# Modulation units two at a time between the mixer's projections, in a fused two-model forward pass

## The reference

```python
mod = jax.nn.silu(c) @ w_ada[l] + b_ada[l]
sh1, sc1, g1, sh2, sc2, g2 = jnp.split(mod, 6, axis=-1)
h = modulate(x, norm1_g[l], sh1, sc1)       # rms_norm * (1+sc) + sh
q_a, k_a, v_a, qk_m, v_m, o_m, gates = jnp.split(h @ w_in[l], offs, axis=-1)
attn = head_rms_norm(moba_attention(rope(q_a), rope(k_a), v_a), attn_out_g[l], 8)
q_m, k_m = jnp.split(silu(causal_conv(qk_m, conv_w[l], conv_b[l])), 2, axis=-1)
hm = mlstm_chunkwise(q_m, k_m * dh ** -0.5, v_m, i_pre, f_pre)  # num / max(|den|, exp(-m))
hm = head_rms_norm(hm, mlstm_out_g[l], 4) * sigmoid(o_m)
x = x + g1 * (concatenate([attn, hm]) @ w_out[l])
h2 = modulate(x, norm2_g[l], sh2, sc2)
x = rms_norm(x + g2 * hier_moe(h2, ...), norm_f_g)   # top group of 4, top 2 of its 8 experts
for i in range(2):                                   # the second model's layers
    x = x + gate1 * (diff_attention(h) if i == 0 else axial_gqa(h))
    x = x + gate2 * ((silu(h @ w_gate) * (h @ w_up)) @ w_down)
return rmsnorm(x, final_g)
```

## Time and profile before

| what | value |
|---|---|
| median of 3 runs | 1418.47 us |
| the profiled execution | 1423.29 us, of which the span of its instructions is 1421.5 us |
| PE busy | 1170.6 us (82% of the span), 9691 instructions |
| PEld busy | 931.3 us (66%) |
| DVE, ACT busy | 617.6 us (43%), 527.2 us (37%) |
| chain that ended last | PE 56%, DMA 22%, DVE 13%, ACT 8%, issue 2% |
| read from memory | 394.97 MB, 279 GB/s over the span |

### The profile page before, as it was taken

How to read it: one execution, slowest core, us unless ns; L and a number is a source line. 1 busy time by engine, 2 the same in 40 slices (tenths; PEclk the granted TensorE clock), 3 DMA queues, 4 the chain that set the end, 5 groups by cost and what they waited for, 6 DMA issues and landing times.

```text
span 1421.5 us, 22433 instructions
## 1 busy us (share of the span) xinstructions
PE 1170.6 (82%) x9691; PEld 931.3 (66%) x9691; DVE 617.6 (43%) x1358; ACT 527.2 (37%) x1154; POOL 0.2 (0%) x4
## 2 busy tenths in 40 slices
PE   4898889866665666665589989999999979999997
PEld 3776666543432444343256758899998748899997
DVE  2386564311110111111045656565555755566554
ACT  3344354211010110101044665555554544555543
POOL 0000000000000000000000000000000000000000
PEclk9899899998888888989799999999999989999999
DMA  9565366999999999999977646645446554654420
GB/s 390 221 245 229 126 283 236 414 428 427 427 427 427 423 427 426 427 426 427 428 314 307 240 163 231 249 178 187 179 148 225 197 230 153 249 191 180 178 89 30
DMA packets 29424, 397.52 MB, mean 280 GB/s; under 512 B 3464, under 2 KB 4872, under 8 KB 5128
## 3 DMA queue, kind: packets, MB, share of 16 engines
q1 hardware_dynamic: 29176, 394.98, 68.9%
q10 hardware_dynamic: 144, 1.05, 0.2%
HBM read 394.97 MB, written 1.05 MB: 279 GB/s over the span
## 4 chain that ended last, share of the span: by engine, by line
PE 56%; DMA 22%; DVE 13%; ACT 8%; issue 2%; SPq 0%; DVEq 0%; ACTq 0%
PE ps L141 56%; DMA ring<-in_w 12%; DMA mem<-in_w 9%; DVE mem L141 7%; DVE memr L141 4%; ACT mem L141 4%; ACT memr L141 3%; DVE small L141 1%; DMA ring<-in_wpk 1%; ACT rowb L141 1%; ACT L141 0%; DVE x L141 0%; DVE mcol L141 0%; SPq L141 0%; ACT small L141 0%
## 5 line engine op out<-in xcount | busy, mean ns | idle before, releaser
L141 PE MATMUL ps<-memr 128*128 128x256 f32 (+1 forms) x4656 | 674.9, 304 | 21.7 <-DVE memr L141 21.7
L141 PEld LDWEIGHTS ps<-memr 128*128 128x128 f32 x4656 | 614.2, 194 | 67.3 <-DVE memr L141 31.6
L141 DVE TENSOR_TENSOR memr<-ring,memr 128x512 fp32r<-128x512 f32 x432 | 292.1, 690 | 240.8 <-ACT memr L141 238.5
L141 PE MATMUL ps<-mem 128*32 128x256 f32 (+4 forms) x2232 | 266.2, 407 | 108.8 <-DMA ring<-in_w 44.4
L141 ACT ACTIVATE memr<-ring 128x512 fp32r<-128x512 f32 x432 | 262.0, 627 | 238.6 <-PE ps L141 225.1
L141 PEld LDWEIGHTS ps<-mem 128*32 128x32 f32 (+2 forms) x2232 | 170.8, 147 | 173.9 <-issue 109.5
L141 ACT ACTIVATE mem<-ps 128x256 f32<-128x256 f32 (+5 forms) x307 | 120.9, 407 | 420.5 <-PE ps L141 419.6
L141 PE MATMUL ps<-ring,mem 128*32 128x256 f32 x1536 | 142.6, 433 | 34.8 <-DMA ring<-in_w 25.8
L141 DVE TENSOR_TENSOR mem<-mem,ps 128x256 f32<-128x256 f32 (+1 forms) x76 | 31.8, 418 | 276.5 <-ACT mem L141 276.5
L141 PEld LDWEIGHTS ps<-ring,mem 128*32 128x32 f32 x1536 | 72.9, 124 | 73.9 <-issue 49.7
L141 DVE COPY mem<-ps 32x256 f32<-32x256 f32 (+1 forms) x80 | 37.8, 472 | 110.1 <-PE ps L141 109.1
(11 more groups left out here) (94 smaller groups left out, 402.7 us busy)
## 6 DMA issues: line engine op xcount, KB each, us to landing
ring<-in_wpk SPq DMA_DIRECT2D x87, 2048.0 KB, 7.7
ring<-in_w SPq DMA_DIRECT2D x48, 2048.0 KB, 31.7
mem<-in_w SPq DMA_DIRECT2D x48, 2048.0 KB, 31.5
mem<-in_wpk SPq DMA_DIRECT2D x3, 2048.0 KB, 7.5
ring<-in_wpk SPq DMA_DIRECT2D x2, 1024.0 KB, 5.0
x<-in_x ACTq DMA_DIRECT2D x1, 1024.0 KB, 5.4
out_dram<-mem SPq DMA_DIRECT2D x4, 256.0 KB, 2.2
cst<-in_cst SPq DMA_DIRECT2D x1, 976.0 KB
```

The lines of the kernel that those rows point to most:

```text
L141: ins = o[1](*o[2], **o[3])
```

## The change

It alters several places of the program at once, and what is computed stays the same.

- **Start.** x is loaded in two halves by SP, ahead of the units; columns, constants and positions by ACT. The norm of x stands before the first modulation unit on PE, the tables of the rotary embedding are made at once, the late constants are issued after units 4 and 5, and slabs of `I3` are staged between the steps of `modulate_x`.
- **Gates.** The eight gate columns are the weights (two blocks of 4, at 0 and 32 of 36 columns) and h is what moves; the transposes of the result are gone, and the gates stand behind projection `I4`.
- **Convolution.** Its first tap runs on ACT.
- **mLSTM.** No reciprocal: the numerator is squared, the square of the denominator times EPS is added to the mean, and ln and exp give the scale for both.
- **Modulation units.** Two (one before `I6` and before the second half of the output product) stand between projections; units 10 and 11 of layer 0 and 2 and 3 of layer 1 are used before the output product ends, none in the routing. The list of units follows.
- **Squares.** Before the norms that follow the two feed-forwards, and the second norm after the experts, DVE adds the squares and PE folds two.
- **Third layer.** Half of q is projected first, then k and v; norm and rotary run one after another in `side`, ACT sums the squares; modulation units 6, 7, 8 are loaded after the first unit of the output product, and 7 and 8 are used inside the attention.

The diff, cut:

```diff
-        ld_cols = S.dma(sem("s_cols"), cols[:, :], t["cols"])
-        ld_c1 = S.dma(sem("s_c1"), cst[:, 0:256], t["cst1"])
-        ld_x = A.dma(sem("s_x"), x[:, :, :], t["x"])
+        ld_cols = A.dma(sem("s_cols"), cols[:, :], t["cols"])
+        ld_c1 = A.dma(sem("s_c1"), cst[:, 0:K1], t["cst1"])
+        ld_pos = A.dma(sem("s_pos"), posi[:, :], t["pos"])
+        s_x = [sem("s_x0"), sem("s_x1")]
+        ld_x = [S.dma(s_x[j], x[:, 4 * j:4 * j + 4, :], t["x"][:, 4 * j:4 * j + 4, :]) for j in range(2)]
         s_ld2 = sem("s_ld2")
 
...
         mixed(ada(0, 0), ada(0, 2), (U_IN + 3, 8), ada(0, 1), ada(0, 3), (U_IN + 4, 8), ada(0, 4), (U_IN + 6, 8), ada(0, 5),
-              (U_IN + 5, 8), ada(0, 6), (U_IN, 8), ada(0, 7), (U_IN + 1, 8), (U_IN + 2, 8), ada(0, 8), ada(1, 0), (U_OUT, 8),
-              ada(0, 9), ada(1, 1), (U_OUT + 1, 8), ada(0, 10), ada(0, 11), ada(1, 2), ada(1, 3))
+              ada(0, 6), (U_IN + 5, 8), ada(0, 7), ada(0, 8), (U_IN, 8), ada(0, 9), ada(0, 10), (U_IN + 1, 8), ada(0, 11),
+              ada(1, 0), (U_IN + 2, 8), ada(1, 1), ada(1, 2), (U_OUT, 8), ada(1, 3), (U_OUT + 1, 8))
         for e in range(32):
             for name in ("w1", "w3", "w2"):
                 units.append(t[name][e])
         moe_last = len(units)
-        mixed((U_AQKV, 8), ada(1, 4), (U_AQKV + 2, 8), ada(1, 5), (U_AQKV + 4, 8), ada(1, 6), ada(1, 7), (U_AQKV + 1, 8),
-              ada(1, 8), ada(2, 2),
-              (U_AQKV + 3, 8), ada(2, 3), (U_AQKV + 5, 8), ada(1, 9),
-              ada(1, 10), (U_AWO, 8), ada(1, 11), (U_AWO + 1, 8), ada(2, 0), ada(2, 1))
+        mixed((U_AQKV, 8), ada(1, 4), (U_AQKV + 2, 8), ada(1, 5), (U_AQKV + 4, 8), ada(1, 6), ada(1, 7),
+              (U_AQKV + 1, 8), ada(1, 8), (U_AQKV + 3, 8), ada(2, 2), (U_AQKV + 5, 8), ada(2, 3),
+              (U_AWO, 8), ada(1, 9), ada(1, 10), (U_AWO + 1, 8), ada(1, 11), ada(2, 0), ada(2, 1))
         for i in range(2):
             mixed(*[(U_FIN + 11 * i + n, 8) for n in range(11)],
                   *[(U_FOUT + 6 * i + n, 8 if n < 5 else 4) for n in range(6)])
             if i == 0:
-                mixed(ada(2, 4), ada(2, 5), (U_BQKV + 2, 8), (U_BQKV, 8), (U_BQKV + 1, 8), ada(2, 6), ada(2, 7), ada(2, 8),
-                      (U_BWO, 8), ada(2, 9), (U_BWO + 1, 8), ada(2, 10), ada(2, 11))
+                mixed(ada(2, 4), ada(2, 5), (U_BQKV, 8), (U_BQKV + 2, 8), (U_BQKV + 1, 8), (U_BWO, 8), ada(2, 6), ada(2, 7),
+                      ada(2, 8), (U_BWO + 1, 8), ada(2, 9), ada(2, 10), ada(2, 11))
...
+            def add(self, c, src, recs):
+
+                z = 3 if c == 0 else c % 3
+                r = A(sc.activation, sq[:, z, :], src, ACT.Square, after=list(recs) + sq_free[z])
+                if c == 0:
+                    self.acc = r
+                    return
+                self.flush()
+                self.held = (z, r)
+
+            def flush(self):
+                if self.held:
+                    z, r = self.held
+                    self.acc = V(vt.tensor_tensor, sq[:, 3, :], sq[:, 3, :], sq[:, z, :], ALU.add, after=[r, self.acc])
+                    sq_free[z] = [self.acc]
+                    self.held = None
+
+            def pair(self):
+
+                z, r = self.held
+                self.todo = [(sq[:, 3, :], sq_free[3], self.acc), (sq[:, z, :], sq_free[z], r)]
+                self.n, self.last = 0, 1
...
+                        if norm and nt > 8:
+                            norm.add(n, xT[:, n, :], [out[n]])
+                            if n == 7:
+                                norm.pair()
+                                norm.fold()
+                        elif norm:
...
+        x_r = {c: ld_x[c // 4] for c in range(8)}
+        rope_v = rope_tables()
+        nm = Norm()
+        for c2 in range(0, 8, 2):
+            nm.square(c2, xT[:, c2:c2 + 2, :], [ld_x[c2 // 4]], 2)
+            if c2:
+                nm.fold()
+                nm.fold()
+        use_tables(SILU)
+        rope_r = [A(sc.activation, cc, cc, ACT.Sin, after=[rope_v]), A(sc.activation, ssn, ssn, ACT.Sin)]
+        rB_r = nm.close()
+        ada_mm(0, 0)
+        ada_copy()
+        ada_mm(0, 2)
+        ada_copy()
+        ada_close(True)
+        ld_cst = ld_rows = late_loads()
...
+        def gate_weights():
+            r0 = [V(vt.tensor_scalar, w, bc(cst[:, K_ONE:K_ONE + 36], [128, 8, 36], 1), 0.0, None, ALU.mult, after=[ld_c1])
+                  for w in wg2]
+            for j in range(2):
+                d = slice(32 * j, 32 * j + 4)
+                r = A(sc.activation, wg2[0][:, :, d], wgt[:, :, 4 * j:4 * j + 4], ACT.Copy, after=r0 + [ld_rows])
+                wg_r.append(V(vt.tensor_tensor, wg2[1][:, :, d], wgt[:, :, 4 * j:4 * j + 4], wg2[0][:, :, d], ALU.subtract,
+                              after=[r]))
+
         def gates():
-            r = A(sc.activation, wgs[:, 0, :, :], wgt[:, :, :], ACT.Copy, after=[ld_rows])
-            wr = V(vt.tensor_tensor, wgs[:, 1, :, :], wgt[:, :, :], wgs[:, 0, :, :], ALU.subtract, after=[r])
             b, ps, fr = PB.take()
-            for tt in range(2):
-                s = slice(128 * tt, 128 * tt + 128)
-                for k in range(8):
-                    r = mm3(ps[:, 8 * tt:8 * tt + 8], (h2[0][:, k, s], h2[1][:, k, s]), (wgs[:, 0, k, :], wgs[:, 1, k, :]),
-                            k == 0, k == 7, after=fr + [wr, h2_r[k]])
-            rg = V(vt.tensor_copy, gtok, ps[:, 0:16].rearrange("p (t n) -> p t n", t=2), after=[r])
-            PB.give(b, [rg])
-            return rg
-
-        def gate_rows(rg):
-            b, ps, fr = PB.take()
-            for g in range(2):
-                for tt in range(2):
-                    r = T(te.transpose, ps[0:4, 256 * g + 128 * tt:256 * g + 128 * tt + 128], gtok[:, tt, 4 * g:4 * g + 4],
-                          ident, after=fr + [rg])
+            for k in range(8):
+                r = mm3(ps[0:36, 0:256], (wg2[0][:, k, :], wg2[1][:, k, :]), (h2[0][:, k, :], h2[1][:, k, :]),
+                        k == 0, k == 7, after=fr + wg_r + [h2_r[k]])
+            return b, ps, r
...
-                dr = V(vt.reciprocal, dd, dd, after=[dr])
-                hr = V(vt.tensor_tensor, kmt, heads4(ps[:, :]), heads4(dd), ALU.mult, after=[dr, r] + done)
-                PB.give(b, [hr])
+                nr = A(sc.activation, EMb, ps[:, :], ACT.Copy, after=[r, dr])
+                PB.give(b, [nr])
+                sr = A(sc.activation, kmt, heads4(EMb), ACT.Square, after=[nr] + done)
+                dr = A(sc.activation, dd, dd, ACT.Square, scale=float(EPS ** 0.5), after=[dr])
                 yield
-                r = A(sc.activation, dd, kmt.rearrange("p h n -> p (h n)"), ACT.Square, after=[hr])
                 b, ps, fr = PB.take()
-                r = mm(ps[:, :], ones, dd, True, True, after=fr + [r])
+                r = mm(ps[:, :], ones, kmt.rearrange("p h n -> p (h n)"), True, True, after=fr + [sr])
                 yield
-                r = A(sc.activation, EMb, ps[:, :], ACT.Ln, bias=EPS, scale=1.0 / 128, after=[r, dr])
-                PB.give(b, [r])
-                r = A(sc.activation, EMb, EMb, ACT.Exp, scale=-0.5, after=[r])
+                dr = V(vt.scalar_tensor_tensor, out=dd, in0=ps[:, :], scalar=1.0 / 128, in1=dd, op0=ALU.mult, op1=ALU.add,
+                       after=[r, dr])
+                PB.give(b, [dr])
+                r = A(sc.activation, dd, dd, ACT.Ln, after=[dr])
+                r = A(sc.activation, dd, dd, ACT.Exp, scale=-0.5, after=[r])
                 yield
-                r = V(vt.tensor_tensor, kmt, kmt, heads4(EMb), ALU.mult, after=[r])
+                r = V(vt.tensor_tensor, kmt, heads4(EMb), heads4(dd), ALU.mult, after=[r])
...
-        rg = gates()
-        jobs += [(gate_rows(rg), 2), (rope_tables(), 3), (conv(0, copies), 1)]
+        gate_weights()
+        jobs += [(conv(0, copies), 1)]
         side.append(work())
         bk, r = project_T(h2, h2_r, 256, 128)
-        jobs.append((conv(1, conv_copy(1, bk, r)), 1))
+        copies = conv_copy(1, bk, r)
+        jobs += [(conv(1, copies), 1), (gate_rows(*gates()), 1)]
+        if not side:
+            side.append(work())
         ada_unit(0, 4)
         bk, r = project_T(h2, h2_r, 256, 128)
         for j in range(2):
@@ -1052,10 +1094,11 @@
             PB.give(bk[j][0], [ra])
             om_r.append(V(vt.tensor_scalar, o, o, 0.5, 0.5, ALU.mult, ALU.add, after=[ra]))
         ada_unit(0, 5)
+        ada_unit(0, 6)
         vm_r += project(h2, h2_r, lambda tt, ps, dep: A(sc.activation, vm[:, tt, :], ps[:, :], ACT.Copy, after=dep))[0]
-        ada_unit(0, 6)
-        while any(4 + h not in conv_r for h in range(4)):
-            next(side[0])
+        ada_unit(0, 7)
+        ada_unit(0, 8)
+        drain()
...
-        ada_unit(0, 7)
+        ada_unit(0, 9)
+        ada_unit(0, 10)
         rope_unit(kst, kT, kt_r, 1.0)
+        ada_unit(0, 11)
+        ada_unit(1, 0)
```

(33 more changed lines are left out.)

175 lines of the change are left out of this document (88 added, 87 removed).

## The result

The changed kernel takes **1384.43 us**, the median of four runs (1380.57 to 1388.81); the kernel before took 1421.24 us on the same chip. The ratio is 0.974, with a 95% interval of 0.970 to 0.979: faster by 36.8 us. The forecast was 1373 us with a range of 1360 to 1394. The direction, most places and the range were right; the time is 11 us above the forecast, the gain 36.8 us in place of 45.5, and several terms were wrong in size, not all in the same direction.

What follows compares the result with a forecast made beforehand. DMA bounds the experts' window, PE what follows. Terms: -29 us up to the experts' end, -6.3 squares, -11 third layer, sum -46: 1377 us profiled; the profile stood 4.8 above the median, so 1373 us, range 1360 to 1394.

Steps and rivals of the forecast that it cites:

- A: Start: folds run before the first modulation unit lands, so the first projection starts sooner; -6 us, bounds -4 and -9.
- B: Gates: 24 matmuls of 256 columns replace 48 small ones, upper clock expected; -10 us, bounds -6 and -11.
- C: mLSTM norm: waits for the reciprocal shrink (-8) and the lower clock behind them goes (-5.4); -13.4 us, bounds -9 and -14.
- D: Four more modulation units ahead of the routing cost 10.1 us, attention's start returns 3.5; +6.6 us, bounds +5 and +9.
- E: Routing: counts, logits and norm no longer stand behind modulation units; -7 us, bounds -10 and +3.
- F: Squares: six folds fewer on PE at each of three places, 0.35 us each; -6.3 us, bounds -6.3 and 0.
- G: Third layer: output product's first unit loads before three modulation units, ending ACT's 11.12 us wait; -11 us, bounds -3 and -14.
- the stream: Experts' loads: all eight places are loaded by the release, so the stream starts anew then; +1 us.
- The rule for the experts' end: The experts end 434 us after the first expert's weights are released; bringing that forward moves the end as much.
- Rival 4: Between projections, ACT is held by loads not yet landed, 10.2 us per hold, +71 in all: 1444 us; chance 0.04.
- Rival 1: Routing runs at the lower clock, costing up to 12.7 us; routing term about +3, time 1383 us; chance 0.15.
- two signs of being wrong: ACT waits for DMA between projections, or PEclk near 0.5 for more than 7 us before the first expert.

Runs made afterwards that it cites:

- gates_only: Kernel before with only the gate columns made weights and h moving in 256 columns, at their old place: 1416.19 us, ratio 0.9965.
- norm_only: Kernel before with only the new mLSTM norm (ACT copies and squares the numerator, no reciprocal): 1413.54 us, ratio 0.9946.
- units_back: Changed kernel with the first part's modulation units at their old places and in their old order of loads: 1390.71 us, ratio 0.9796.
- folds_back: Changed kernel with eight folds of squares on PE at each of the three places, as before: 1388.1 us, ratio 0.9787.
- third_back: Changed kernel with the third layer's loads, projections, norm, rotary and places of units 6 to 8 as before: 1394.24 us, ratio 0.9832.
- two paddings: Changed kernel with 30 unused matmuls on PE, between the output product's halves (1401.83 us) or ahead of the sixth expert group (1385.39 us).
- units_att: units_back with two modulation units moved from ahead of the attention to after its first and second step: 1387.75 us, ratio 0.9780.
- norm_att: norm_only with two modulation units moved from ahead of the attention to after its first and second step: 1410.9 us, ratio 0.9923.
- gate_first: Changed kernel with the gate chain ahead of the convolution's second half, two steps a slab: 1380.87 us, ratio 0.9741.
- both: gate_first with modulation unit 3 of layer 1 used in PE's gap ahead of the routing's logits: 1376.0 us, ratio 0.9675.

## Why the forecast was right, and where not

| step | forecast, us | measured, us | from |
|---|---|---|---|
| A start | -6 | -6.3 | first projection 30.52 to 24.19 |
| B gates | -10 | -5.0 | gates_only, ratio; gates at their old place |
| C mLSTM norm | -13.4 | -7.7 | norm_only, gather and ratio |
| D and E, modulation units and routing | +6.6 - 7 | -6.3 | units_back, medians |
| F squares | -6.3 | -3.7 | folds_back, medians |
| G third layer | -11 | -9.8 | third_back, medians |
| sum | -46 (with +1 for the stream) | -38.8 | the kernels' medians differ by 36.8 |

Term by term this mixes runs in the kernel before with runs in the changed one. The two profiled executions can be laid side by side up to the release as well; where units have moved, 2.5 us each are counted in the forecast:

| stretch of PE, up to (before; now) | forecast, us | traces, us |
|---|---|---|
| first projection (30.52; 24.19) | -6 | -6.3 |
| second half of `I3` (45.32; 40.21) | 0 | +1.2 |
| behind the gates (85.47; 68.19) | -10 | -12.2 |
| mLSTM's first transposes (110.11; 101.27), two units more | +5 | +8.4 |
| attention (188.13; 172.00), one unit more | -10.9 | -7.3 |
| end of the attention's start (217.75; 200.34), two more | +1.5 | -1.3 |
| release (273.41; 247.28), five fewer | -9.5 | -8.7 |
| sum | -29.9 | -26.1 |

**Right.** The rule for the experts' end: 434.6 us after the release, and two paddings show it. So is the restart of the stream as no loss worth speaking of. The first projection, both waits at the ones matmuls, the end of the long stretch at the lower clock at the gates, and the third layer's hold fell as described. G is the one large term behind the experts, and by the rows it is a load order more than arithmetic.

**C was too large**, by 5.7 us, **and B by 5 in gates_only**, for two reasons. First, each removed wait made room for a smaller one behind it that I had not looked for: 1.97 us at the denominators, 1.60 at the slabs behind the gates. I had asked what stands behind the removed wait on the same engine, but not whether DVE, late by as much as before, would be reached sooner. Second, I counted the clock as if each stretch at the lower level belonged to its wait and would vanish with it. norm_only, gates_only, units_att and norm_att each show it at a later place: 10.3 us in place of 3.4 in the attention's start, 6.9 us in the routing. Half of each such stretch is time, so C lost 2.9 us of its 10.6 to this. B's shortfall is that of gates_only alone: in the changed kernel, with the gates behind `I4`, its stretch gave 12.2 us, more than forecast, and the next one cost 3.4 us more than forecast, since PE waits 4.50 us there for the gate chain. Whether the kernel or the single execution decides how long such a stretch lasts is not settled; norm_only, gates_only and units_back, which all have the wait of 2.65 us, have some 10 us there, and the kernel before has 3.4.

**D and E were too small**, by 6 us. Up to the attention three more units cost 7.6 us, 2.5 each as I took, with 1.6 us of a longer wait and a shorter stretch at the lower clock in it; but the two inside the attention paid for themselves and 4 us more, because in the kernel with B and C the attention's start would have been slow for 10 us, not for the 3.4 that the trace before showed. The errors in C and in D are the same error seen from two sides, and they cancel in part.

**Rival 4** (ACT held by loads) happened once, at a pair: 3.56 us. Its price was not 10.2 but at most the 4.50 us of PE's wait, and gate_first removes the wait and leaves the hold. The forecast had it as "ACT may wait up to 4 us, I take 0": the size was right, but behind ACT stood the gate chain, which the change itself had moved there. The load fit says how long the hold is, the queue behind it what it costs. **Rival 1** happened in part: logits, transposes and gather ran 1.4, 1.7 and 2.0 us longer, yet E as a whole gave its share (from the issue of the loads at the end of the output product to the release, 242.28 to 273.41 and 222.85 to 247.28 us, 31.1 against 24.4: -6.7 against -7), since the waits it removes are longer.

**F** gave 3.7 us of 6.3 by the medians. The forecast took six folds off PE at each place and no wait for what replaces them; in the changed kernel PE waits up to 1.54 us for the sum. The traces allow 1 to 3 us at each feed-forward and 1.6 at the third place, so how much of the 6.3 is there stays open.

**The signs.** The forecast named two signs of being wrong, and by the first it should have failed: ACT did wait for DMA between the projections, 3.56 us. The second, more than 7 us at the lower clock ahead of the first expert, came too if the 6.9 us in the routing and another 3.4 in the gather are added. The time stayed in the range all the same, so both signs were too strict for what they cost. The sum of the favourable bounds was added up wrongly as well, -63 where its own bounds give -58; nothing else rests on it. The start (A), the convolution's tap and the order of loads in the second layer have no run of their own.

The remaining gap lies in the yardstick. The two profiled executions differ by 42.7 us, against 46 in the forecast: 26.1 up to the release against 29.8 and 16.8 behind the last unit against 17.3. The medians differ by 36.8 only. About 3 us of this is that the profiled execution of the changed kernel was quick behind the experts, 696.9 us where four others took 699.5 to 700.4; with theirs, F and G together are worth 13.3 to 14.2 us and not 16.8. I had set the profiled execution of the kernel before 4.8 us above its median and so took 1377 to 1373; with all runs of the result that median is 1421.24, and the changed kernel's own profile stands 3.9 us under its median. Against scatter of this size one profiled execution fixes a time to no better than 4 us.

## What to carry to other kernels

When a stretch is bound by a stream of loads with all places in use, find the release that starts it and cost everything ahead of it against that one moment; pad with useless work on both sides to prove it. When you remove a wait, price it by itself and take the clock gained behind it at half or less: of the 10 to 13 us at the lower clock that norm_only, gates_only, units_att and norm_att each took away, 3.6, 6.6, 3.6 and 6.4 us stayed away up to the gather. Units of independent work were worth more inside the late waits of such a stretch (two of them brought 4 us in the attention's start) than ahead of it, where each cost 2.5. And before you put work behind a staging instruction, ask whether its load has landed: a hold of 5.5 us cost PE under 1 us here, with nothing urgent behind it, and one of 11 us cost it over 6.

## What the runs showed of the hardware

- One wait is not followed by one fixed loss of clock: around the same 2.65 us of idle PE the granted clock was 0.50 for 3.4 us in one trace and for 10.3 us in another.
- The clock also fell with hardly any idle PE: in `both` at 224.6 us, behind 3.86 us of unbroken 40-column matmuls (the idle time before them was 0.6 us, 6 us earlier), and it was 0.53 for 3.5 us. With the 8-column matmuls of the gates, which a wait of 2.10 us came before, it stayed at 0.51 for 13.8 us in which PE was never idle.
- A matmul of fp32 with 256 columns takes 0.22 us for each of its two records at the upper clock when sixty stand in a row (13.22/60), and a fold of squares between slabs costs PE some 0.24 to 0.35 us, not the 0.59 to 0.70 that the length of its row shows, since the rows overlap.
